# Rotary partner rows loaded from DRAM instead of computed with a rotation matrix

## The reference

```python
def _rotary(x, pos):
    half = ROT_DIM // 2                       # 8 of the 64 channels
    inv = ROPE_THETA ** (-jnp.arange(half, dtype=jnp.float32) / half)
    ...
    x1 = x[..., :half]
    x2 = x[..., half:ROT_DIM]
    rot = jnp.concatenate([x1 * cos - x2 * sin, x2 * cos + x1 * sin], axis=-1)
    return jnp.concatenate([rot, x[..., ROT_DIM:]], axis=-1)

dq = _rotary(b_q.reshape(b, t, DIFF_HEADS, 2, HEAD_DIM), qpos1)
dk = _rotary(b_k.reshape(b, t, DIFF_HEADS, 2, HEAD_DIM), qpos1)
```

## Time and profile before

| what | value |
|---|---|
| median of 3 runs | 2890.88 us (2887.85 to 2892.25) |
| profiled execution, span | 2887.4 us |
| PE busy | 2757.3 us, 95% |
| PE weight load busy | 2574.4 us, 89% |
| DVE busy | 1620.5 us, 56% |
| ACT busy | 745.3 us, 26% |
| POOL busy | 243.9 us, 8% |
| mean granted clock of PE | 0.989 |
| chain that ended last | PE 80%, DVE 8%, ACT 3%, DVEq 3%, DMA 3%, issue 2% |
| transfers | 290.26 MB, mean 101 GB/s |

### The profile page before, as it was taken

How to read it: one execution, slowest core, us unless ns; L and a number is a source line. 1 busy time by engine, 2 the same in 40 slices (tenths; PEclk the granted TensorE clock), 3 DMA queues, 4 the chain that set the end, 5 groups by cost and what they waited for, 6 DMA issues and landing times.

```text
span 2887.4 us, 63061 instructions
## 1 busy us (share of the span) xinstructions
PE 2757.3 (95%) x26472; PEld 2574.4 (89%) x26472; DVE 1620.5 (56%) x2991; ACT 745.3 (26%) x1779; POOL 243.9 (8%) x423
## 2 busy tenths in 40 slices
PE   7999999999999989999989999999999999999998
PEld 6877889999999789999988778899999997899997
DVE  5444655666664266664374455556666633766633
ACT  1143443222232330000112433432223324200001
POOL 1221112000000100000002211110000000000000
PEclk9999999999999999999999999999999999999999
DMA  4453436222263133323225434452223532223231
GB/s 136 129 144 103 143 104 169 72 72 64 74 175 103 44 92 88 88 87 86 78 85 136 119 114 137 100 158 72 72 64 111 156 92 68 77 88 89 85 88 58
DMA packets 420762, 290.26 MB, mean 101 GB/s; under 512 B 38544, under 2 KB 386352, under 8 KB 420352
## 3 DMA queue, kind: packets, MB, share of 16 engines
q1 hardware_dynamic: 398496, 228.64, 28.8%
q0 software_dynamic: 21984, 57.59, 6.3%
HBM read 232.12 MB, written 54.07 MB: 99 GB/s over the span
## 4 chain that ended last, share of the span: by engine, by line
PE 80%; DVE 8%; ACT 3%; DVEq 3%; DMA 3%; issue 2%; ACTq 0%; SPq 0%
PE PS L740 35%; PE PS L809 9%; PE PS L1112 8%; PE PS L1045 7%; PE PS L718 4%; PE PS L1256 2%; DMA U<-gate_scratch 2%; ACT U L1371 1%; PE PS L855 1%; PE PS L1086 1%; ACT U L1374 1%; PE PS L759 1%; PE PS L1176 1%; PE PS L891 1%; PE PS L970 1%
## 5 line engine op out<-in xcount | busy, mean ns | idle before, releaser
L740 PE MATMUL PS<-U_r,WHI 128*128 128x272 f32 x2656 | 474.7, 289 | 11.3 <-DVEq L2283 7.5
L1374 ACT COPY U<-PS 128x272 f32<-128x272 f32 (+8 forms) x758 | 265.0, 374 | 747.0 <-PE PS L1112 140.0
L1858 DVE CAST WHI<-ring 128x1024 fp32r<-128x1024 f32 (+1 forms) x240 | 164.1, 684 | 472.8 <-PE PS L740 365.7
L740 PEld LDWEIGHTS PS<-U_r,WHI 128*128 128x128 f32 x2656 | 386.3, 188 | 16.8 <-DVEq L2283 11.7
L740 PE MATMUL PS<-brT_r,WHI 128*128 128x272 f32 x1728 | 357.4, 288 | 1.0 <-DVEq L1869 1.0
L740 PE MATMUL PS<-U_r,WLO 128*128 128x272 f32 x1696 | 350.3, 288 | 0.0
L740 PE MATMUL PS<-hT_r,WHI 128*128 128x272 f32 x1696 | 349.7, 288 | 0.0
L1868 DVE TENSOR_TENSOR WLO<-ring,WHI 128x1024 fp32r<-128x1024 f32 (+1 forms) x240 | 289.9, 1208 | 19.4 <-issue 1.3
L740 PE MATMUL PS<-brT_r,WLO 128*128 128x272 f32 x1344 | 278.2, 288 | 0.0
L809 PE MATMUL PS<-U_r,WHI 128*128 128x272 f32 x832 | 261.7, 314 | 12.4 <-ACT U L1374 12.3
L740 PEld LDWEIGHTS PS<-brT_r,WHI 128*128 128x128 f32 x1728 | 271.5, 188 | 1.9 <-DVEq L1869 1.9
(11 more groups left out here) (337 smaller groups left out, 4285.7 us busy)
## 6 DMA issues: line engine op xcount, KB each, us to landing
ring<-in_w_in_dram SPq DMA_DIRECT2D x126, 512.0 KB, 4.3
ring<-in_w_ffn_in_dram SPq DMA_DIRECT2D x88, 512.0 KB, 3.8
ring<-in_w_ffn_out_dram SPq DMA_DIRECT2D x32, 448.0 KB, 3.7
proj_scratch<-U POOLq DMA_DIRECT2D x104, 136.0 KB, 2.1
U<-proj_scratch SPq DMA_DIRECT2D x48, 272.0 KB, 4.3
ring<-in_w_branch_dram SPq DMA_DIRECT2D x48, 256.0 KB, 3.2
gate_scratch<-U POOLq DMA_DIRECT2D x88, 136.0 KB, 3.1
U<-gate_scratch SPq DMA_DIRECT2D x44, 272.0 KB, 2.9
```

The source lines that it names most:

```text
L740: ins = mm(PS[:, 2 * q + h, 0:HT], w, half(x, h), start=(first and k == 0 and n == 0), stop=(last and k == kn - 1 and n == len(terms) - 1))
L1374: return act.copy(out, in_)
L1858: copy(hi, src)
```

## The change

The rotation matrix `rot` and its products on PE go, and with them `df_rot`. For q and k there is a buffer of partner rows each: DPART[0] is a new one, DPART[1] is DTMP. SP loads into them, for each of the four groups of eight rotary channels, the eight partner rows straight from `proj_d`: four transfers of 8 rows for q and four for k in each head, between the loads of DK and DVR. The sine table carries the sign. The q transfers wait until the head before has been rotated (`df_rotated`), the k transfers until the head before has its sum (`df_sum`); in (0,0) those for k wait for `fx_rows` instead. DVE zeroes the buffers once a layer, DPART[0] in the input projection and DPART[1] at the start of fox iteration 3, waits for the five loads and the partner rows, and multiplies partner rows by the sine in one instruction of 544 columns. PE no longer waits for `df_rs` before a head; the order of its late pieces stays, with the wait for `df_loaded` behind the first (in (0,0) the second), and the wait for `df_evac` moves to the first score tile. The work area grows by 472 columns, and an unused semaphore goes.

```diff
-for _name, _w in (("ident", 128), ("stack", 192), ("bdones", 128), ("rot", 128), ("mfox", 128), ("mdiff", 128),
+for _name, _w in (("ident", 128), ("stack", 192), ("bdones", 128), ("mfox", 128), ("mdiff", 128),
...
-        rope[b:b + 8, 1] = np.sin(ang)
+        rope[b:b + 8, 1] = np.sin(ang) * (-1.0 if b in (0, 64) else 1.0)
...
+        DPART = (cv(T), DTMP)
...
-                        sp.wait_ge(fx_rows, l * 2 + min(it, 1) + 1)
+                        sp.wait_ge(fx_rows, l * 3 + min(it, 1) + 1)
...
                         load(DQ[h], rows(R_DQ)).then_inc(s, 16)
                         load(DK[h][:, 0:T], rows(R_DK)).then_inc(s, 16)
+                        for i, r in enumerate((R_DQ, R_DK)):
+                            if (it, h) != (0, 0):
+                                if i == 0:
+                                    sp.wait_ge(df_rotated, l * 8 + 2 * (2 * it + h))
+                                else:
+                                    sp.wait_ge(df_sum, l * 4 + 2 * it + h)
+                            elif i == 1:
+                                sp.wait_ge(fx_rows, l * 3 + 3)
+                            for b in (0, 8, 64, 72):
+                                r0 = r + it * 256 + P * h + (b ^ 8)
+                                load(DPART[i][b:b + 8, :], proj_d[r0:r0 + 8, :]).then_inc(df_part[i], 16)
                         load(DVR[h], rows(R_DV)).then_inc(s, 16)
...
                         s0 = 4 * 12 + 14 * (2 * it + h)
+                        late(s0)
                         if (it, h) == (0, 0):
-                            late(s0)
+                            late(s0 + 1)
+                            pe.wait_ge(fx_evac, l * 8 + 10)
+                        else:
+
+                            pe.wait_ge(df_put, g * 18 + 9 * h)
                         pe.wait_ge(df_loaded[h], (g + 1) * 16 * 5)
-
-                        for i, src in enumerate((DQ[h], DK[h])):
-                            if i == 0 and (it, h) != (0, 0):
-
-                                pe.wait_ge(df_rs, g * 2 + h)
-                            if i == 1:
-                                pe.wait_ge(df_evac, g * 2 + h + 1)
-                            r = 2 * i if (it, h) == (0, 0) else 2 - 2 * i
-                            for s in range(2):
-                                ins = mm(PS[:, r + s, 0:HT], const("rot"), half(src, s), start=True,
-                                         stop=True)
-                            ins.then_inc(df_rot, 1)
...
+                            if p == 0:
+
+                                pe.wait_ge(df_evac, g * 2 + h + 1)
...
+                        dve.memset(DPART[0], 0.0)
                         dve.drain().then_inc(fx_rows, 1)
...
+                    if it == 3:
+                        dve.memset(DPART[1], 0.0)
+                        dve.drain().then_inc(fx_rows, 1)
...
-                            dve.wait_ge(df_rot, g * 4 + 2 * h + i + 1)
-                            r = 2 * i if (it, h) == (0, 0) else 2 - 2 * i
-                            for s in range(2):
-                                tt(half(DTMP, s), PS[:, r + s, 0:HT], half(ROPE[:, 1, :], s), ALU.mult)
+                            if i == 0:
+                                dve.wait_ge(df_loaded[h], (g + 1) * 16 * 5)
+                            dve.wait_ge(df_part[i], (g * 2 + h + 1) * 64)
+                            part = DPART[i]
                             tt(x[:, 0:T], x[:, 0:T], ROPE[:, 0, :], ALU.mult)
+                            tt(part, part, ROPE[:, 1, :], ALU.mult)
                             dve.drain()
-                            tt(x[:, 0:T], x[:, 0:T], DTMP, ALU.add)
+                            tt(x[:, 0:T], x[:, 0:T], part, ALU.add)
```

More of the change, by code:

```diff
@@ L132, in constants @@
     put("bdones", np.kron(np.eye(2), np.ones((64, 64))))
[L133 to L138, removed]
     q, k = np.arange(P)[:, None], np.arange(P)[None, :]
@@ L201, in build_program @@
         PLF = sb("PLF", [P, 4, 8])
-        NU = 26000
+        NU = 26472
         U, UR = twins("U", [P, NU])
@@ L360, in build_program @@
         vec_loaded, vec_turned, vec_ready = sem("vec_loaded"), sem("vec_turned"), sem("vec_ready")
-        sq_act, sq_dve, sums_done, rstd_ready, h_ready = (
-            sem(n) for n in ("sq_act", "sq_dve", "sums_done", "rstd_ready", "h_ready"))
+        sq_act, sums_done, rstd_ready, h_ready = (
+            sem(n) for n in ("sq_act", "sums_done", "rstd_ready", "h_ready"))
         est_stored, est_free = [sem(f"est_stored{i}") for i in range(4)], sem("est_free")
@@ L376, in build_program @@
         rope_loaded = sem("rope_loaded")
+        df_part = [sem("df_part_q"), sem("df_part_k")]
         df_loaded = [sem("df_loaded0"), sem("df_loaded1")]
         df_stored = [sem("df_stored0"), sem("df_stored1")]
-        (df_rot, df_rotated, df_scores, df_max, df_exp, df_comb, df_turned, df_put, df_out, df_sq, df_sum, df_rs,
-         df_evac) = (sem("df_" + n) for n in ("rot", "rotated", "scores", "max", "exp", "comb", "turned", "put",
+        (df_rotated, df_scores, df_max, df_exp, df_comb, df_turned, df_put, df_out, df_sq, df_sum, df_rs,
+         df_evac) = (sem("df_" + n) for n in ("rotated", "scores", "max", "exp", "comb", "turned", "put",
                                              "out", "sq", "sum", "rs", "evac"))
```

## The result

The changed kernel takes 2902.53 us (median of 4 runs, 2901.57 to 2905.65), the kernel before 2890.51 beside it. The ratio is 1.0040, 95% interval 1.0027 to 1.0054: slower by 0.4%, where 2905 and +0.5% were forecast. Its profiled execution has a span of 2899.6 us, 12.2 more than before; PE's busy time fell by 6.7 us, less than the 14.7 that the removed products had taken (1.84 in each of eight heads), and its idle time grew by 18.9.

A forecast was written before the change was run, and what follows sets the result against it. PE bounds the kernel, busy 95%. Seams +6.25, first head -1.9 and fill +0.5 a layer, twice, give +9.7; clock +4 makes +13.7 on the 2887.4 span, plus 3.5 to the timed median: 2905 us, range 2893 to 2918.

The forecast's parts named there:

- The wait on SP: At seams between heads, SP's program order holds the next head's loads behind df_sum: data 7.15 us after the sum.
- Four small issues: On SP after df_sum, four k partner transfers at 0.48 us each, 1.9 us, ahead of DVR, DPK and DVT.
- DVT from issue to landing: Last of three loads at a seam: 4.2 us from issue to landing, with ends of 3.2 and 6.1.
- The step that called DVE's strand the later one: At the seams, DVE takes 5.4 us from data to rotated-k transposes, PE's own strand 4.7, so DVE ends later.
- The first heads: First head of each layer has no df_sum ahead; rotated-k transposes come earlier: -1.9 us a layer.
- The fills: Zeroing DPART[0] in the input projection costs 0; zeroing DPART[1] ahead of the fourth fox pair's scale, +0.5 us a layer.
- The clock: Half-rate stretch on PE after each seam's standstill: 0.7 us a seam, six seams, +4 us.
- The third rival: Low clock over PE's seam strand and score tiles: 2 to 3 us a seam, 2913 to 2919 us; chance 0.15.
- Quick landing: At the seams, DVT lands in 3.2 us without clock loss: 2892 to 2895 us, no measurable change; chance 0.14.
- PE's work alone: At the seams, loads come early enough that only PE's removed work counts: faster, 2874 us; chance 0.04.
- The point from which it was to decide: At the seams, data earlier than some 4.7 us after df_sum, where the layer breaks even, make the kernel faster.
- Dear transfers: At the seams, small transfers take 1 us of SP each or DVT lands at 6.1: +12, 2917 us; chance 0.10.

The follow-up runs named there:

- the seams filled: Changed kernel plus five idle PE products at each seam, ahead of PE's wait for the loads: 2900.70 us, ratio 1.0038.
- the kernel with eight transfers: Changed kernel with each of the four k partner transfers of a head cut in two of four rows: 2917.75 us, ratio 1.0087.
- the first repair: Changed kernel with a head's eight partner transfers and their waits moved behind the loads of DVR, DPK and DVT: 2881.42 us, ratio 0.9967.
- the four versions with the loads out of the way: Changed kernel with partner transfers moved last (2881.42 us), that plus idle seam products (2893.34), squares put in DVR (2880.00), or both moves and DPART[1]'s fill moved (2883.08).
- both filled: Changed kernel plus five idle PE products at each seam and one inside each head ahead of the first value products: 2895.01 us, ratio 1.0009.

## Why the prediction was right

**The wait on SP** was the cause at every seam, as forecast. The total lies nearer than its parts, which erred both ways; that is luck:
- Four small issues: 0.33 us each (L504: 0.263 to 0.354, median 0.295, and 0.04 between them), not the 0.48 taken from wider loads. 1.3 us in place of 1.9. The step was the choice of the nearest row: the bound below, 0.37, was not low enough either, while the kernel before has a load of a single row, L484, at 0.25 us, which would have bounded it.
- DVT from issue to landing: 4.4 us in the median, 4.0 to 4.6 at the six seams, against 4.2 (the 5.3 in the rows below is a first head, which does not wait for it). The estimate from loads of other sizes held: from DVR's issue to the last landing it took 4.8 to 5.5 us, forecast 5.1. The 3.8 us that the prediction takes from the Trainium skill's page (DMA: Bandwidth & Descriptors, "Anatomy of one DMA") is too short at all six; the page gives that fit for transfers issued by GpSimd, and these are issued by SP. The data were there 6.2 to 6.9 us behind the sum, against 7.15. The rows of the changed kernel:

```profile
L508 SPq DMA_DIRECT2D U<-in_cache_diff_v_dram x8: 502/502/507, 246.4 to 1832.4; - x8
...
DMA to landing us min/median/max: 4.0/4.4/5.3
```

- From the data to L950: 6.1 to 6.5 us, against 5.4 and 0.7 for the clock, 6.1. *The step that called DVE's strand the later one holds only at full clock.* DVE's rotation took its 5.0 us, but PE's own strand from the value transposes, 4.7 us at full clock, took 6.0 to 6.3 with a stretch at half rate in it, and set L950. With the seams filled, DVE released L950 again, 5.1 us after the data. So DVE's strand was taken 0.3 us too long and the clock's price 0.6 too low, and the sum of the two came out near for that reason.
- PE stood 2.3 to 2.9 us before the value transposes, under the 3.5 to 4.5 that the prediction named as a sign: the data came earlier, and PE stood another 0.7 to 0.8 us for ACT's eviction in front of its second late piece, which the sum had not.

Seams in all: +15.9 us, forecast +12.5 and 4.2 for the clock. The stretches of low clock elsewhere (2.5 us less inside the heads, 1.9 more in a fox iteration) were in no sum; they nearly cancel in this pair of executions.

**The first heads** gave 1.84 us a layer, against 1.9. DVE starts without waiting for PE, beside the earlier trace rows:

```profile
280.19 0.72 DVE L2006 TENSOR_TENSOR U<-U 128x544 f32<-128x544 f32 x1 [0.22 <-issue]
...
285.86 0.60 PE L950 MATMUL PS<-CB,U 128*128 128x128 f32 x4
```

**The fills.** The one in the input projection moved the next split by 0.6 us and the one after by nothing: hidden, as argued. The one ahead of the fourth fox pair had no slack, beside the earlier trace rows:

```profile
242.51 0.49 PE L863 MATMUL PS<-U 66*128 66x128 f32 x2 [0.57 <-DVE U L1965]
```

From DVE's last split ahead of it to the next one it takes 0.78 us more in each layer, against 0.5. The weight tiles that left later cost nothing: DVE waits for no tile of the ring in either profile.

**The clock** was in the sum at +4, and the forecast's 0.7 a seam was too low: the filled seams gave back 7.1 us behind the data, 1.2 a seam. Inside the heads it was no loss against the kernel before, which had more such stretches itself. The third rival (2 to 3 us a seam) was right in kind: PE's strand at half clock decides, as it said, at half its price. It came nearer in the kernel with eight transfers, at 3.1 us for each seam into (1,0) and 1.2 to 1.9 at the others. The length of the standstill alone does not decide that: it was 3.8 us both at (1,0) and at (0,1) there.

**The rivals.** Quick landing: no, nothing landed under 3.96 us. PE's work alone: not in this kernel, but the first repair made it true: with the loads out of the way 2881 us, where the rival's sum was 2874. It missed ACT's eviction, which makes the seam 8.6 us and not 8.1, and the split ahead of DVE's rotation at the seam into (1,0), 10.0 and not 8.1. The point from which it was to decide, data 4.7 us after the sum, is misplaced: by the prediction's own terms the seams into (0,1) and (1,1) break even there, but the layer, with the first head's gain and the fill, breaks even at 5.5. No run here settles it. Dear transfers: no, they were cheaper than taken.

## What to carry to other kernels

A queue that issues in program order, as SP's does here, makes every transfer behind a waiting one wait too: before a load is put into such a queue with a wait of its own, list what stands behind it and who needs that first, and put it last. The new buffer's other use decides when the wait ends; giving the late use another dead buffer was worth as much as the order. Work taken off the bounding engine pays in full only where no other strand ends later; behind a late load it pays by what it shortens between the load and the next wait. Both can be read from one seam of the trace.

## What the hardware showed that was not expected

- A standstill of 0.54 us of PE, ahead of the first value products, was followed by a stretch at the lower of the two clock levels (0.57 in the mean of the four microseconds above) in some heads and not in others, with the same rows around it: in none to four of the eight heads of a trace. With one idle product in its place it came in none of the sixteen heads of two traces, so the standstill is its cause. What decides between two equal standstills is not shown here.
- Filling the seams alone took the heads with such a stretch from one to four. That the stretches moved there from the seams is not shown: the four versions with the loads out of the way and no product added inside the heads have two to four, the kernel before has three, and one of the four is the first head of a layer, with no filled seam in front. With both filled, the clock was 1.00 throughout the stage.
- SP's time for an issue hardly goes with the bytes: 0.29 us for 8.7 KB in four rows, 0.30 for 17 KB in eight (0.33 with the 0.04 between them), and 0.34 for DVR, 272 KB in 128 rows (0.43 for DK, which has the same shape).
